# First input transposed as it lands, gates read with a zero-step stationary operand, and two mixers' steps in a new order

## The reference

```
for i in range(4):
    x = x + 0.5 * swiglu(rmsnorm(x, ffn1_norm[i]), ffn1_w_gu[i], ffn1_w_down[i])
    h = rmsnorm(x, mix_norm[i])
    m = (gated_deltanet, stick_breaking_attention, dsa_sparse_attention, gated_deltanet)[i](h, ...)
    x = x + m
    x = x + 0.5 * swiglu(rmsnorm(x, ffn2_norm[i]), ffn2_w_gu[i], ffn2_w_down[i])
```

## Time and profile before

| | |
|---|---|
| median of 3 runs | 2981.58 us (2978.01 to 2983.11) |
| the profiled execution | 2981.7 us |
| its span | 2979.6 us |
| PE busy | 2898.6 us (97%) |
| DVE busy | 1826.8 us (61%) |
| ACT busy | 1604.8 us (54%) |
| POOL busy | 403.3 us (14%) |
| mean granted TensorE clock | 0.995 |
| DMA | 575.07 MB, 193 GB/s over the span |

### The profile page before, as it was taken

How to read it: one execution, slowest core, us unless ns; L and a number is a source line. 1 busy time by engine, 2 the same in 40 slices (tenths; PEclk the granted TensorE clock), 3 DMA queues, 4 the chain that set the end, 5 groups by cost and what they waited for, 6 DMA issues and landing times. The chain is left out here.

```text
span 2979.6 us, 36498 instructions
## 1 busy us (share of the span) xinstructions
PE 2898.6 (97%) x14562; PEld 2455.8 (82%) x14562; DVE 1826.8 (61%) x2206; ACT 1604.8 (54%) x2014; POOL 403.3 (14%) x624
## 2 busy tenths in 40 slices
PE   7999899999999999989999998999999999999998
PEld 6888788888988888868888888888888788888787
DVE  5658566565666556476556486556575655675655
ACT  5447764454454454465444476744475564466453
POOL 1204312112002112001202115021000020000020
PEclk9999999999999999999999999999999999999999
DMA  8754248677547767537768643276555597645684
GB/s 248 239 194 129 70 142 243 212 226 229 177 147 235 229 209 244 177 100 215 237 200 245 199 142 112 85 239 220 186 162 172 180 280 232 189 155 174 212 274 158
DMA packets 396394, 575.07 MB, mean 193 GB/s; under 512 B 19745, under 2 KB 248225, under 8 KB 396225
## 3 DMA queue, kind: packets, MB, share of 16 engines
q1 hardware_dynamic: 372544, 509.80, 54.3%
q0 software_dynamic: 23680, 62.95, 6.9%
HBM read 540.16 MB, written 32.51 MB: 192 GB/s over the span
## 5 line engine op out<-in xcount | busy, mean ns | idle before, releaser
L630 DVE TENSOR_TENSOR lo<-raw,hi 128x2048 fp32r<-128x2048 f32 (+1 forms) x479 | 1074.4, 2255 | 720.8 <-ACT hi L612 720.8
L612 ACT ACTIVATE hi<-raw 128x2048 fp32r<-128x2048 f32 (+2 forms) x489 | 912.4, 1872 | 717.0 <-DMA raw<-in_ffn_w_gu 296.0
L426 PE MATMUL ps<-hi,xh 128*128 128x512 f32 (+1 forms) x2208 | 864.1, 391 | 2.8 <-DVE xl L716 2.3
L428 PE MATMUL ps<-hi,xl 128*128 128x512 f32 (+1 forms) x2208 | 858.8, 389 | 0.0
L427 PE MATMUL ps<-lo,xh 128*128 128x512 f32 (+1 forms) x2208 | 858.6, 389 | 0.0
L426 PEld LDWEIGHTS ps<-hi,xh 128*128 128x128 f32 x2208 | 415.4, 188 | 88.1 <-DVE lo L630 3.4
L428 PEld LDWEIGHTS ps<-hi,xl 128*128 128x128 f32 x2208 | 415.2, 188 | 86.0
L427 PEld LDWEIGHTS ps<-lo,xh 128*128 128x128 f32 x2208 | 415.4, 188 | 83.5
L426 PE MATMUL ps<-hi,hhh 128*128 128x512 f32 x704 | 275.2, 391 | 0.0
L427 PE MATMUL ps<-lo,hhh 128*128 128x512 f32 x704 | 274.3, 390 | 0.0
L428 PE MATMUL ps<-hi,hhl 128*128 128x512 f32 x704 | 274.3, 390 | 0.0
(11 more groups left out here) (438 smaller groups left out, 3393.0 us busy)
## 6 DMA issues: line engine op xcount, KB each, us to landing
raw<-in_ffn_w_gu SPq DMA_DIRECT2D x352, 512.0 KB, 4.9
raw<-in_ffn_w_down SPq DMA_DIRECT2D x80, 1024.0 KB, 5.3
raw<-in_w_ff SPq DMA_DIRECT2D x64, 1024.0 KB, 6.1
raw<-in_w_in SPq DMA_DIRECT2D x60, 1024.0 KB, 5.2
raw<-in_gdn_w_in SPq DMA_DIRECT2D x32, 1024.0 KB, 5.8
turned<-hhf POOLq DMA_DIRECT2D x88, 256.0 KB, 5.3
hhr<-turned POOLq DMA_DIRECT2D x352, 64.0 KB, 4.3
raw<-in_sb_w_in SPq DMA_DIRECT2D x12, 1024.0 KB, 5.1
```

The source lines that it names most:

```text
L426: e.matmul(o, a1, r1, start=kk == 0, stop=False)
L428: i = e.matmul(o, a2, r1, start=False, stop=kk == kts - 1)
L612: k.e.activation(k.m.hi[q % RING][:, 0:n], k.m.raw[q % RING][:, 0:n], ACT.Copy).then_inc(*k.up("act_piece_hi", ("hi", q)))
L630: k.e.tensor_tensor(m.lo[i][:, 0:n], m.raw[i][:, 0:n], m.hi[i][:, 0:n].bitcast(F32), ALU.subtract).then_inc(*k.up("dve_piece_lo", ("split" ...
```

## The change

It has four parts.

- The start: SP issues the identity alone first, then pieces 0 and 1 in halves of two k-tiles with the FFN gains between them, then piece 2, and only then the rest of the constants, vectors and rows (`const`), then pieces 3 and 4. ACT issues x as four quarters of 256 KB on its own queue. PE runs 9 transposes of the identity into a spare bank when the identity is there, transposes the first four blocks of x, runs 4 more such transposes, and starts. ACT and DVE split pieces 0 and 1 by k-tile (512 columns), each k-tile followed by its block of `xh` or `xl`. The squares and the root for the norm become script steps of their own in the first FFN's new script, and only the root waits for `const`.
- The gates: the decay product reads `G` with a step of zero along the stationary operand's columns. POOL's copies (L1664) are gone.
- `GDN_SCRIPT` has a new order (both GDN stages).
- In `SB_SCRIPT` the first `W` comes before `x1`.

```diff
...
-        at = lambda p: min(len(self.pieces), p + 1 + min(AHEAD, p + 1)) if p >= 0 else 1
+        at = lambda p: max(FINE, min(len(self.pieces), p + 1 + min(AHEAD, p + 1)))
...
                     k.wait_ge(*b.before)
-                k.wait_ge("split", p)
+                k.wait_ge(*(("split", p, j) if p < FINE else ("split", p)))
...
 def tensor_x1(k, si):
+    if not si.g:
+        return tensor_first_x(k, 1)
+def turned_at(g, c):
+    first = c if not g else c // 2 * 2
+    return first, slice((c - first) * S, (c - first + 1) * S)
+def tensor_first_x(k, s):
+    for c in range(4 * s, 4 * s + 4):
+        b = k.take("xT", 0, c)
+        k.wait_ge(*b.before)
+        for t in range(2):
+            k.wait_ge("x", 0, t, s)
+            i = k.e.transpose(b.ps[:, t * P:(t + 1) * P], k.m.x[:, t, c * P:(c + 1) * P], k.m.C(C_ID))
+        i.then_inc(*k.up("pe_x_turned", ("xT", 0, c)))
+        k.close(b)
+    yield
...
+def scalar_xh(k, si, c):
+    first, part = turned_at(si.g, c)
+    m, b = k.m, k.bank("xT", si.g, first)
+    k.wait_ge("xT", si.g, first)
+    k.e.activation(m.xh[:, c, :], b.ps[:, part], ACT.Copy, scale=m.col(si.gain + c)).then_inc(
+        *k.up("act_xh", ("xh", si.g, c)))
+def scalar_start(k, plan, si):
+    for s in range(2):
+        for r in range(2):
+            k.e.dma_start(k.m.x[:, r, 512 * s:512 * s + 512], k.t["x"][0, r * P:(r + 1) * P, 512 * s:512 * s + 512]).then_inc(
+                *k.up(f"dma_x{2 * s + r}", ("x", 0, r, s), ("res", 0, r, s), by=16))
+    for c in range(8):
+        q, j = c // 4, c % 4
+        k.wait_ge("landed", q, j // 2)
+        k.e.activation(k.m.hi[q][:, 512 * j:512 * j + 512], k.m.raw[q][:, 512 * j:512 * j + 512], ACT.Copy).then_inc(
+            *k.up("act_piece_hi", ("hi", q, j)))
+        k.wait_ge("gains")
+        scalar_xh(k, si, c)
 def scalar_turned_x(k, si, s):
-    e, m, g = k.e, k.m, si.g
-    for a in (4 * s, 4 * s + 2):
-        b = k.bank("xT", g, a)
-        k.wait_ge("xT", g, a)
-        for j in range(2):
-            e.activation(m.xh[:, a + j, :], b.ps[:, j * S:(j + 1) * S], ACT.Copy, scale=m.col(si.gain + a + j)).then_inc(
-                *k.up("act_xh", ("xh", g, a + j)))
+    g = si.g
+    for c in range(4 * s, 4 * s + 4):
+        scalar_xh(k, si, c)
...
 def scalar_x1(k, si):
-    return scalar_turned_kept(k, si.g, 1) if si.before else scalar_turned_x(k, si, 1)
+    return iter((None,)) if not si.g else scalar_turned_kept(k, si.g, 1) if si.before else scalar_turned_x(k, si, 1)
...
+def scalar_first_rstd(k):
+    scalar_squares(k, 0, 0)
+    yield
+    scalar_squares(k, 0, 1)
+    yield
+    k.wait_ge("const")
+    scalar_rstd(k, 0)
+    yield
+def vector_first_rstd(k):
+    yield
+    yield
+    vector_sumsq(k, 0)
+    yield
 def vector_sumsq(k, g):
+def vector_xl(k, si, c):
+    first, part = turned_at(si.g, c)
+    m, g, b = k.m, si.g, k.bank("xT", si.g, first)
+    k.wait_ge("xh", g, c if not g else first + 1)
+    k.e.scalar_tensor_tensor(m.xl[:, c, :], b.ps[:, part], m.col(si.gain + c), m.xh[:, c, :].bitcast(F32), ALU.mult, ALU.subtract).then_inc(
+        *k.up("dve_xl", ("xl", g, c), *([b.read] if c % 2 or not g else [])))
+def vector_start(k, plan, si):
+    m = k.m
+    for c in range(8):
+        q, j = c // 4, c % 4
+        part = slice(512 * j, 512 * j + 512)
+        k.wait_ge("hi", q, j)
+        k.e.tensor_tensor(m.lo[q][:, part], m.raw[q][:, part], m.hi[q][:, part].bitcast(F32), ALU.subtract).then_inc(
+            *k.up("dve_piece_lo", ("split", q, j)))
+        k.wait_ge("gains")
+        vector_xl(k, si, c)
 def vector_turned_x(k, si, s):
-    e, m, g = k.e, k.m, si.g
-    for a in (4 * s, 4 * s + 2):
-        b = k.bank("xT", g, a)
-        k.wait_ge("xh", g, a + 1)
-        for j in range(2):
-            c, i = a + j, b.ps[:, j * S:(j + 1) * S]
-            e.scalar_tensor_tensor(m.xl[:, c, :], i, m.col(si.gain + c), m.xh[:, c, :].bitcast(F32), ALU.mult, ALU.subtract).then_inc(
-                *k.up("dve_xl", ("xl", g, c), *([b.read] if j else [])))
+    g = si.g
+    for c in range(4 * s, 4 * s + 4):
+        vector_xl(k, si, c)
     if s == 1:
...
+FFN_FIRST_SCRIPT = """
+W x1 W squares W squares squares gate flip W W gate W W W W flip gate W turn flip W gate flip W W W W W W W
+turn W gate W W turn flip W W W gate W W flip turn W gate W W W W W W gate flip W W W W flip W gate turn flip
+gate W W W W turn W W flip turn turn W gate W flip W W W turn W W turn turn W W W W out W W W W W W W W W next
+W out out W W
+"""
...
 def ffn_script(plan, si):
-    return (FFN_LAST_SCRIPT if si.after else FFN_SCRIPT).split()
+    return (FFN_LAST_SCRIPT if si.after else FFN_SCRIPT if si.g else FFN_FIRST_SCRIPT).split()
...
 GDN_SCRIPT = """
-clear x1 rbc W c3 W c0 rbc W E ba W E W W gates gates E W gates W E c2 gates W W W nk gates gates W c2 c0 E W
-nk nk W c1 nk E nk kT c0 c2 W nk c0 c2 c1 c3 E W c1 c3 W c1 E W inv c3 E kT W E W W inv gates W W W W W W c0 W
-c3 c2 E c1 c0 W c2 E c0 nq W Z W c2 W nq nq c2 c0 W nq nq nq c0 c2 qk c1 c2 c3 sv c1 c3 W Z c0 c1 rows rows c1
-c0 c3 rows c1 c3 rows c2 c0 gate c1 c3 a0 qk c1 c2 a0 a0 a1 a0 c3 a0 qk qk a1 c3 a0 a0 a1 W a1 a1 a1 W W a1 W
-W out W W next out W out
+c2 c3 clear x1 rbc W W W rbc E E W ba W W W gates W gates E gates E gates W W W gates W nk gates c2 E W nk nk
+W c0 nk c0 E c2 c0 nk W c1 nk c2 W c0 c3 c3 c3 c1 E c1 W inv W c1 W E kT kT W E nq W E W inv W W W c0 gates c3
+c2 E c1 W W W c0 E W nq c2 Z c0 W W nq c0 W nq nq nq c2 sv W c0 c3 Z W c1 c0 c2 c1 rows rows c3 rows c2 c3 c1
+rows c2 c1 c0 gate c2 c3 c1 qk c0 qk c1 a0 c3 c2 a0 a0 c1 a0 a1 a0 qk c3 a1 a0 c3 a1 qk a1 a0 a1 a1 W W W a1
+out W W W W next out W out
...
         yield
-        tensor_four(k, n("decay"), at(2), lambda h: C(C_UT), n("gb"))
+        tensor_four(k, n("decay"), lambda h: r["G"][:, t, h0 + h:h0 + h + 1].to_broadcast([P, P]), lambda h: C(C_UT), ("g", g))
...
         t, h0, s = g4 // 2, 4 * (g4 % 2), r["slot"][g4]
-        k.wait_ge("g", g)
-        e.tensor_copy(s[2], r["G"][:, t, h0:h0 + 4].unsqueeze(2).to_broadcast([P, 4, P])).then_inc(*k.up("pool_gdn", ("gb", g, g4)))
...
 SB_SCRIPT = """
-x1 W rbc W E W W W E rbc E W E W W W E W W heads W heads W heads W E heads W E heads E W heads W heads W W v W
+W x1 rbc W E W W W E rbc E W E W W W E W W heads W heads W heads W E heads W E heads E W heads W heads W W v W
...
+def tensor_warm(k, b, n, *events):
+    for _ in range(n):
+        i = k.e.transpose(b.ps[:, 0:P], k.m.C(C_ID), k.m.C(C_ID))
+    i.then_inc(*k.up("pe_warm", *events))
 def tensor_program(k, plan, infos):
-    k.wait_ge("const")
-    run(["x0"], {"x0": tensor_turn_x(k, 0, 0)})
+    b = k.take("warm")
+    k.wait_ge("id")
+    tensor_warm(k, b, 9)
+    for _ in tensor_first_x(k, 0):
+        pass
+    tensor_warm(k, b, 4, b.read)
+    k.close(b)
     for si, nxt in zip(infos, infos[1:]):
+        if si.g == 1:
+            k.wait_ge("const")
 def scalar_program(k, plan, infos):
-    scalar_split(k, plan, 0)
-    k.wait_ge("const")
-    run(["x0"], {"x0": scalar_turned_x(k, infos[0], 0)})
+    scalar_start(k, plan, infos[0])
 def vector_program(k, plan, infos):
-    vector_split(k, plan, 0)
+    vector_start(k, plan, infos[0])
+    for si, nxt in zip(infos, infos[1:]):
+        if si.g == 1:
+            k.wait_ge("const")
+        VECTOR[si.name](k, plan, si, nxt, SCRIPT[si.name](plan, si))
+def pool_program(k, plan, infos):
     k.wait_ge("const")
-    run(["x0"], {"x0": vector_turned_x(k, infos[0], 0)})
-    for si, nxt in zip(infos, infos[1:]):
-        VECTOR[si.name](k, plan, si, nxt, SCRIPT[si.name](plan, si))
-def pool_program(k, plan, infos):
...
+def sync_fine(k, plan, p, h):
+    dims, parts = plan.pieces[p]
+    view = k.m.ring(k.m.raw, p, dims)
+    for n, (index, src) in enumerate(parts):
+        k.e.dma_start(view[:, 2 * h:2 * h + 2, n], src[:, 2 * h:2 * h + 2]).then_inc(
+            *k.up(f"dma_fine{2 * p + h}", *([("landed", p, h)] if n == len(parts) - 1 else []), by=16))
...
     e, m, t = k.e, k.m, k.t
-    sync_piece(k, plan, 0)
-    e.dma_start(m.const[:, :], t["consts"]).then_inc(*k.up("dma_const", by=16))
-    e.dma_start(m.vec[:, :], t["vecs"]).then_inc(*k.up("dma_const", by=16))
-    e.dma_start(m.row[:, :], t["rows"].partition_broadcast(P)).then_inc(*k.up("dma_const", by=16))
-    x = [(n, 0, r, s) for n in ("x", "res") for r in range(2) for s in range(2)]
-    e.dma_start(m.x[:, :, :], t["x"][0].rearrange("(t p) d -> p t d", p=P)).then_inc(*k.up("dma_const", ("const",), *x, by=16))
-    for p in range(1, RING):
+    e.dma_start(m.const[:, 0:P], t["consts"][:, 0:P]).then_inc(*k.up("dma_id", ("id",), by=16))
+    sync_fine(k, plan, 0, 0)
+    e.dma_start(m.vec[:, 0:V_CONV], t["vecs"][:, 0:V_CONV]).then_inc(*k.up("dma_gains", ("gains",), by=16))
+    sync_fine(k, plan, 0, 1)
+    for h in range(2):
+        sync_fine(k, plan, 1, h)
+    sync_piece(k, plan, 2)
+    e.dma_start(m.const[:, P:], t["consts"][:, P:]).then_inc(*k.up("dma_const", by=16))
```

(4 more changed lines are left out.)

6 lines of the change are left out of this document (4 added, 2 removed).

## The result

The changed kernel takes 2962.94 us, the median of 5 runs (2958.92 to 2970.71), against 2981.58 us for the kernel before in the same comparison (5 runs, 2978.01 to 2990.18): a ratio of 0.9931, 95% interval 0.9915 to 0.9948. That is 18.6 us faster. Forecast was 2953, so 28.5 us faster; the time lies inside the range of 2941 to 2967. Run once more, in a second comparison (experiment 11), the changed kernel was 13.9 us faster than the kernel before.

The account below looks back on a forecast made before the run. PE, busy 97% of the span, bounds the kernel; only its 81 us idle and half-clock time can be won. Start 9.2, GDN 18.4 (19.4 less one), stick-breaking 0.9: 28.5 us off 2981.7, so 2953; 8 in 10 for 2941 to 2967.

Parts of the forecast that it names:

- signs of being wrong: DVE's second turn as late as before, new waits pulling the clock down in the stages, or zero-step loads well over 0.17 us.
- Start: Start of the kernel: the third piece's first matmul comes at 22.2 instead of 31.44, a gain of 9.2 us.
- Gates: Decay product in each GDN stage: POOL's copies cost PE 4.0 us a stage in wait and slow matmuls; all goes.
- norm waits: GDN stage before the inversion: two PE waits before norm sums, 1.8 us, go; the second stage has only one.
- As far as the inversion: First GDN stage up to the inversion: 1.0 of 5.8 us kept, bounds 0 to 5.
- The two new waits: Before the inversion: PE waits 1.9 us at the third k-norm sum and 2.5 at k k^T of chain 3.
- The inversion: First GDN stage, around and behind the inversion: waits and slow matmuls of 8.2 us all go, bounds 3 and 8.2.
- Second stage: Second GDN stage: 9.7 us from the same waits and longer half clock, plus about 0.5 from its first part.
- The 3.9 us for a clock that stays at half for longer: Second GDN stage: loss from half clock around 1828 to 1834, counted within its 9.7 us.
- Tail: GDN steps after the last z step: chain 1 has seven steps there instead of five; gain 0, bounds -3 and +3.
- Stick-breaking: Stick-breaking stage: the first `W` covers a PE wait before a transpose of x, a gain of 0.9 us.
- the gain stays at the start: Rival, chance 0.2: DVE or POOL bound the GDN stages, removed waits come back; 3 us a stage, 2965.6 in all.

Follow-up runs that it names:

- experiment 11: The changed kernel run again, unedited, in a second comparison against the kernel before: 2967.14 us against 2981.04, ratio 0.9950.
- experiments 1 to 4: Kernel before with only the start, only the gates, only the new `GDN_SCRIPT`, or gates and script: 2973.04, 2982.98, 2978.30 and 2976.70 us.
- experiment 8: Changed kernel with 12 of the 13 early transposes left out and the old stick-breaking script: 2963.96 us.

## Why the prediction was off

Its mechanisms were right for the start and for stick-breaking, and the largest step of the gated-delta part failed. That the time lies inside the stated range is partly luck: the second comparison's median, 2967.14, lies just outside it. Two of the forecast's own signs of being wrong are there: new waits pull the clock down in the stages (2.21 us for `ga`, 3.39 for the copy), and DVE's second turn is only 2.0 us earlier against the stage's start.

- *Start, 9.2 forecast, 8.3 measured.* Half a piece landed at 7.33 (the ACT row), not at the 6.2 taken; the first product stood at 9.22, not 8.5, and nine matmuls ran at the lower clock, not 6. ACT and DVE set the third piece, as forecast, at 23.1 instead of 22.2. But they are themselves held by PE's slow matmuls, through the second x transposes. The kernel with only the start agrees with that: its clock rose before the first product, and it has the second transposes at 12.18 instead of 13.89, the third piece at 21.40 instead of 23.12. Of these 1.7 us it gives 0.9 back at piece 4, whose split came 0.9 us late (PE's next row after 32.19 stands at 33.27), a place that the forecast called close, without a loss. So the entry of the gated-delta stage varies by no more than 1.2 us: 193.1 to 193.6 in the five profiles whose clock rose before the first product, 193.7 to 194.2 in the four others.
- *Gates, 4.0 a stage.* The wait for POOL did go, and the zero-step load cost nothing. But the 4.81 us that the forecast took for POOL's work were 0.61 of copy behind two splits of DVE, and in the changed kernel the half clock only moved ahead of the decay product. By itself that is worth 2.5 to 2.9 us a stage: the idle time is kept, the 1.4 us of half clock come back later. With the new script it is worth 0.4 and 0.1, since that script hides the copies. The sum kept 1.0 of it and the norm waits together, so this term did no harm.
- *As far as the inversion, 1.0 forecast.* Idle time fell by 2.3 us. The two new waits are there: k k^T waits 1.7 for the scaled k (2.5 forecast). The third norm sum does not wait; the product behind `ga` (L1266) waits 2.2 us where it waited 1.4. DVE turned 5.9 us earlier against the stage's start, where 4.2 was forecast.
- *The inversion, 8.2 forecast, the failed step.* "By the hand schedule PE meets all of these without a wait. I take all 8.2 for the first stage." The schedule moved DVE's work forward and priced DVE's instructions there at their undisturbed length. In fact POOL's splits, of which one lay beside two splits of DVE before, came to lie beside the last convolution step, two of them. PE still waits 1.15 (1.03 before), 0.88 (1.9) and 3.39 (3.68), and the clock still falls. 1.0 us of idle time was won for 8.2. The kernels with other sets of splits show that the contention is the cause of 2.1 us of the third wait and of the fall of the clock behind it, together 3.7 to 4.1 us a stage. With one split a stage left to POOL PE still waits 1.14, 0.90 and 1.26 us there, so "without a wait" was wrong apart from the contention too. The stage's total was there to be had all the same: with the same script and one split a stage left to POOL the stages give 10.1 and 11.0 us, against the 9.2 and 10.2 forecast, part of it in the tail, for which the forecast had nothing.
- *Second stage, 10.2.* It gave 5.0, for the same reason: its wait of 3.39 us and the fall of the clock behind it repeat themselves. The 3.9 us for a clock that stays at half for longer were also read off one execution: with the same script, the kernel with only the start has the lower granted clock in its first stage.
- *Tail, 0.* It gave 1.6 of idle time in the first stage; chain 1's later steps cost PE nothing that shows in it.
- *Stick-breaking, 0.9.* 0.65, shown in both directions.

Of the rivals, "the gain stays at the start" had the right mechanism, a wait that comes back behind the next instruction, at 3 us a stage and 2965.6; the outcome lies between it and the forecast. It was given 0.2 and deserved more, since the row that spoke for it stood in the earlier trace rows: DVE's two splits at 8.88 us for two beside POOL. The forecast read that row as a price of that place, and not as a price that goes wherever POOL splits; the earlier trace rows had the other side of it, POOL's copy at 4.81 us.

## What to carry to other kernels

When a hand-made order is changed, move every engine's work on the same clock: a pair of engines that slow each other belongs in the schedule as one resource, wherever the two meet. Before an instruction's length is taken for its work, compare it with others of the same size: behind the copy of 4.81 us came three of 0.61. A wait counted with the slow matmuls behind it is worth its idle part only, until the waits behind it are known to leave the clock up. And work given to an idle engine is no gift: POOL's five splits a stage took 4.6 us each, DVE's own 2.3, and with four of the five taken back the stages ran 5.6 and 5.9 us shorter. The fifth did pay: with it taken back too they were 3.9 and 5.3 us longer again.

## What the runs showed of the hardware

- *An instruction of DVE with two inputs from SBUF stands still while POOL splits.* In the changed kernel POOL works from 300.69 to 310.00; DVE's six instructions, begun at 301.95, end at 311.87. The first of them ends at 305.56, where POOL goes from one split to the next (305.28), and the other five take 2.06 at the undisturbed length: they ran after POOL was done. With one split (301.02 to 305.60) they end at 307.86, 2.26 later. Before, DVE's and POOL's splits begin together at 301.25; POOL's takes 6.73 us, 2.15 more than the 4.58 of the split above, which is about the length of DVE's first, and DVE's second ends 2.14 after POOL's. The row of before:

```profile
301.26 6.73 POOL L648 TENSOR_TENSOR lo<-raw,hi 128x2048 fp32r<-128x2048 f32 x1
```

  Instructions of DVE that read a bank keep their length: beside the split of POOL from 329.95 to 334.50 the changed kernel has

```profile
333.16 0.69 DVE L1632 COPY sy<-ps 128x512 f32<-128x512 f32 x1 [4.20 <-PE ps L613]
```

  while `qkv<-qkv,sy` (L1624), 0.69 us by itself, takes 3.91 at 316.88, beside the split from 315.66 to 320.24. It works the other way too: POOL's copy of 0.61 us took 4.81 behind two splits of DVE, and did not come in between the two (experiments 1 to 4).

  The Trainium skill (SBUF — State Buffer, SBUF: two separate sides) says that a DVE instruction with two inputs from that memory and a GpSimd instruction that reads it can't use one shared pair of ports together: whichever starts first holds it for its whole length. The trace agrees, to 0.2 us in each of the three places first named.
- *The clock can rise on transposes alone.* In five of the nine profiles of kernels with the 13 early transposes, one of the changed kernel's two among them, the first product already runs at 0.23 us a matmul; until then PE had done only transposes. In the five kernels without them (the four with the old start, and the one of experiment 8) it never does: the first products are 0.42 or 0.43 us apart. With the start alone:

```profile
7.42 0.60 PE L2926 MATMUL ps<-const 128*128 128x128 f32 x4
9.33 0.47 PE L427 MATMUL ps<-hi,xh 128*128 128x512 f32 x1 [1.30 <-DVE xl L775]
9.64 0.39 PE L428 MATMUL ps<-lo,xh 128*128 128x512 f32 x1
```

  Four take 0.60 us here and 1.06 in the changed kernel's profile, where the clock rose at 13.2. The rule that transposes don't count for the clock (the Trainium skill, TensorE: Matmul & The Clock Gate, Part 4: PE-mode transpose) does not hold in these rows; the measurement decides. What decides between the two moments was not tried.
